# Preparing attention's keys, values and masks inside the retention chunks of a two-block transformer kernel on one Trainium2 core

## The reference

```python
r_q, r_k = rotary(r_q), rotary(r_k)                  # 8 heads of 64
ret = head_group_norm(retention(r_q, r_k, r_v), ret_norm) * silu(r_g)
c_kv, k_pe = rms_norm(d_c, kv_norm), rotary(d_pe)    # latent of 128, shared rotary part of 16
dsa = sparse_attention(q_nope, q_pe, c_kv, k_pe, q_idx, k_idx, w_idx, w_uk, w_uv) * silu(d_g)
x = x + concatenate([ret, dsa]) @ w_out
```

## Time and profile before

| | us |
|---|---|
| three runs: median (lowest to highest) | 2272.81 (2270.8 to 2273.53) |
| the profiled execution, its own time | 2270.93 |
| its span, first to last instruction | 2269.1 |
| outside the span | 1.83 |
| retention block | 85.04 |
| preparation of attention | 32.21 |
| attention's steps up to 2040 us | 140.05 |

### The profile page before, as it was taken

How to read it: one execution, slowest core, us unless ns; L and a number is a source line. 1 busy time by engine, 2 the same in 40 slices (tenths; PEclk the granted TensorE clock), 3 DMA queues, 4 the chain that set the end, 5 groups by cost and what they waited for, 6 DMA issues and landing times. The chain is left out here.

```text
span 2269.1 us, 27732 instructions
## 1 busy us (share of the span) xinstructions
PE 2117.0 (93%) x10549; PEld 1599.9 (71%) x10549; DVE 1278.9 (56%) x2211; ACT 733.0 (32%) x1292; POOL 435.1 (19%) x501
## 2 busy tenths in 40 slices
PE   7998999995969999999999998889999868989998
PEld 4744464484858888888888886856888764658876
DVE  6591895278864333223454324478999577762433
ACT  2222021122113323223444223356121335761415
POOL 2900011042310000000000001223666440300210
PEclk8999999997989999999999999899999889999999
DMA  8543110003233333334434232122211002003101
GB/s 325 155 134 116 42 46 1 0 2 121 75 102 93 93 97 89 90 106 147 121 111 130 81 97 87 58 56 61 66 47 50 20 3 81 2 25 130 51 0 75
DMA packets 187512, 180.59 MB, mean 80 GB/s; under 512 B 12982, under 2 KB 157686, under 8 KB 184074
## 3 DMA queue, kind: packets, MB, share of 16 engines
q1 hardware_dynamic: 184426, 168.61, 23.9%
q0 software_dynamic: 2880, 10.49, 1.2%
q10 hardware_dynamic: 96, 0.02, 0.0%
HBM read 165.18 MB, written 12.60 MB: 78 GB/s over the span
## 5 line engine op out<-in xcount | busy, mean ns | idle before, releaser
L1800 DVE TENSOR_TENSOR ff_part<-ff_raw,ff_part 128x1024 fp32r<-128x1024 f32 (+2 forms) x152 | 164.9, 1085 | 435.5 <-ACT ff_part L1708 435.5
L1708 ACT ACTIVATE ff_part<-ff_raw 128x1024 fp32r<-128x1024 f32 (+2 forms) x152 | 144.0, 948 | 433.4 <-PE ps L1598 430.9
L1596 PE MATMUL ps<-h,ff_part 128*128 128x512 f32 x704 | 275.5, 391 | 4.7 <-DVE ff_part L1800 4.7
L1598 PE MATMUL ps<-h,ff_part 128*128 128x512 f32 x704 | 274.7, 390 | 0.0
L1597 PE MATMUL ps<-h,ff_part 128*128 128x512 f32 x704 | 274.7, 390 | 0.0
L2416 DVE TENSOR_SCALAR_CACHE_REDUCE pj_junk<-NM,prm 128x384 uint8<-128x384 f32 (+1 forms) x186 | 163.7, 942 | 1.1
L1596 PEld LDWEIGHTS ps<-h,ff_part 128*128 128x128 f32 x704 | 132.8, 189 | 32.3 <-DVE ff_part L1800 5.1
L1596 PE MATMUL ps<-pj_part,h 128*128 128x512 f32 x384 | 153.2, 399 | 0.2 <-ACT PJ L2273 0.2
L1597 PEld LDWEIGHTS ps<-h,ff_part 128*128 128x128 f32 x704 | 132.8, 189 | 27.4
L1598 PEld LDWEIGHTS ps<-h,ff_part 128*128 128x128 f32 x704 | 132.6, 188 | 27.6
L1597 PE MATMUL ps<-pj_part,h 128*128 128x512 f32 x384 | 150.4, 392 | 0.0
(11 more groups left out here) (601 smaller groups left out, 4057.7 us busy)
## 6 DMA issues: line engine op xcount, KB each, us to landing
ff_raw<-in_w_ffn_in SPq DMA_DIRECT2D x88, 512.0 KB, 3.7
s_wm<-in_w_mod SPq DMA_DIRECT2D x16, 1024.0 KB, 4.9
pj_raw<-in_w_in SPq DMA_DIRECT2D x64, 256.0 KB, 2.7
ff_raw<-in_w_ffn_out SPq DMA_DIRECT2D x32, 384.0 KB, 3.4
ff_raw<-in_w_ffn_out SPq DMA_DIRECT2D x32, 320.0 KB, 3.0
mod_w<-in_w_mod SPq DMA_DIRECT2D x8, 1024.0 KB, 8.9
mod_x<-in_x SPq DMA_DIRECT2D x8, 512.0 KB, 13.9
w_out<-in_w_out SPq DMA_DIRECT2D x4, 1024.0 KB, 8.7
```

What stands on the lines that cost most here:

```text
L1596: nc.tensor.matmul(out, w[0], x[0], start=first, stop=False)
L1598: return nc.tensor.matmul(out, w[1], x[0], start=False, stop=last)
L1708: nc.scalar.activation(part[s % 2][0][:, 0:n, :], raw[s][:, 0:n, :], ACT.Copy).then_inc(hi, 1)
L1800: v.tensor_tensor(part[s % 2][1][:, 0:n, :], raw[s][:, 0:n, :], part[s % 2][0][:, 0:n, :].bitcast(F32), ALU.subtract).then_inc(lo, 1)
```

## The change

The preparation of attention moves into the retention block.

- At retention's start, PE transposes the attention queries (`turn_queries`) and the latent and rotary part (`turn_latent`) of all 8 tiles. ACT copies the queries out, DVE the latent and rotary part (one copy of 128 x 256 a tile). `intra`, `xi` and the gain row are loaded after the last query transposes, into the `D_Q` slab; `zeta`, `decay`, `w_uv` and the 8 pieces of `w_uk` before them.
- In each chunk PE also makes a value piece (`prepare(2 * i)`, before the state update) and a key piece (`prepare(2 * i + 1)`, after it), through bank 2, and ACT copies each out (`prepared`).
- DVE makes mask 7 before the chunks, then one of nine parts (masks 6, 5 and 4, three each) at the end of each chunk's work, the ninth after the last norm. ACT lowers masks 7, 6 and 5 after chunks 1, 4 and 7, and mask 4 at the block's end.
- The state's decay goes from DVE (one instruction) to ACT (four of 128 x 128).
- Zero-padded queries and values are gone: scores are 8 products on 64 rows, the output's second part 8 products of 64 columns. Keys are weighed by zeta in place, and the norm's squares go into the `R_K` slab.
- In `stage_first_end` pairs of weight loads share a semaphore.

The diff, cut to what the text speaks of:

```diff
             def split(k):
-                act.wait_ge(w_in[k], 32)
+                act.wait_ge(w_in[k // 2], 64)
                 nc.scalar.activation(K.mixed[k][0][:], raw[k][:], ACT.Copy).then_inc(K.pj["hi"], 1)
...
+        link(v.tensor_tensor_scan(run[:, 0:n], flag[:, 0:n], flag[:, 0:n], 0.0, ALU.add, ALU.max))
+    else:
+        link(v.scalar_tensor_tensor(out=run[:, 0:n], in0=run[:, 0:n], scalar=need, in1=flag[:, 0:n], op0=ALU.is_le, op1=ALU.mult))
+        return v.scalar_tensor_tensor(out=x, in0=x, scalar=at, in1=run[:, 0:n], op0=ALU.is_gt, op1=ALU.add)
...
+            sp.dma_start(zeta, I["zeta"]).then_inc(S["const"], 16)
+            sp.dma_start(decay, I["decay"]).then_inc(S["const"], 16)
+            with nc.allow_non_contiguous_dma(reason="latent to partitions"):
+                sp.dma_start(wuv[:], I["w_uv_2"][0].rearrange("h c d -> c h d")).then_inc(S["wuv"], 16)
+            sp.wait_ge(S["clear"], 2)
+            for h in range(AH):
+                sp.dma_start(uk[AD * (h % 2) + PE_D:AD * (h % 2 + 1), h // 2, :], I["w_uk_2"][0, h]).then_inc(S["uk"], 16)
+            sp.wait_ge(S["dqt"], NT)
             sp.dma_start(intra[:], I["intra"].rearrange("p (j a) t -> p j a t", a=2)).then_inc(S["const"], 16)
             sp.dma_start(xi[:], I["xi"]).then_inc(S["const"], 16)
-            sp.dma_start(zeta, I["zeta"]).then_inc(S["const"], 16)
-            sp.dma_start(decay, I["decay"]).then_inc(S["const"], 16)
             sp.dma_start(row[:], I["ret_norm_2"].to_broadcast([P, HALF])).then_inc(S["const"], 16)
...
             def turn(i):
                     pe.wait_ge(S["qkr"], 2 * i)
-                    pe.wait_ge(S["dqr"], i)
-                for b, slab in enumerate((R_Q, R_K, D_Q)):
+                for b, slab in enumerate((R_Q, R_K)):
                     for j in range(J):
                         tr = nc.tensor.transpose(K.bank[b][:, j * P:(j + 1) * P], K.PJ[:, slab, i, j * P:(j + 1) * P], K.ident[:])
                     tr.then_inc(S["tr"], 1)
+            def turn_queries(i):
+                if i >= 4:
+                    pe.wait_ge(S["dqr"], i - 3)
+                for j in range(J):
+                    tr = nc.tensor.transpose(K.bank[2 + i % 4][:, j * P:(j + 1) * P], K.PJ[:, D_Q, i, j * P:(j + 1) * P], K.ident[:])
+                tr.then_inc(S["dqt"], 1)
+
+            def turn_latent(i):
+                if i >= 2:
+                    pe.wait_ge(S["latr"], i - 1)
+                b = K.bank[6 + i % 2]
+                nc.tensor.transpose(b[:, 0:P], K.MS[:, i, 0:LAT], K.ident[:])
+                nc.tensor.transpose(b[:, P:2 * P], K.MS[:, i, M_PE:M_PE + P], K.ident[:]).then_inc(S["turn"], 1)
+
+            def prepare(n):
+                if n:
+                    pe.wait_ge(S["prer"], n)
+                b, m = K.bank[2][:], n // 2
+                if n % 2 == 0:
+                    nc.tensor.matmul(b, latT[:, m * P:(m + 1) * P], wuv[:].rearrange("p h d -> p (h d)"), start=True, stop=True).then_inc(S["pre"], 1)
+                else:
+                    c = slice(m % 2 * HALF, (m % 2 + 1) * HALF)
+                    nc.tensor.matmul(b, ukT[:, m // 2, :], latT[:, c], start=True, stop=False)
+                    nc.tensor.matmul(b, spread[:].rearrange("p a d -> p (a d)"), peT[:, c], start=False, stop=True).then_inc(S["pre"], 1)
+
             turn(0)
+            for i in range(NT):
+                turn_queries(i)
+                turn_latent(i)
+            pe.wait_ge(S["uk"], 16 * AH)
+            pe.wait_ge(S["dqr"], NT)
+            pe.wait_ge(S["latr"], NT)
+            for j in range(J):
+                tr = nc.tensor.transpose(K.bank[2][:, j * P:(j + 1) * P], uk[:, j, :], K.ident[:])
+            tr.then_inc(S["ukr"], 1)
             for i in range(NT):
                 for j in range(J):
-                    mm = nc.tensor.matmul(K.bank[3 + j // 2].rearrange("p (j a t) -> p j a t", j=2, a=2)[:, j % 2], kT[s][:, j, :], qpad[s][:, j, :, :],
-                                          start=True, stop=True)
+                    for a in range(2):
+                        d = slice(RD * a, RD * (a + 1))
+                        mm = nc.tensor.matmul(K.bank[3 + a][:, j * P:(j + 1) * P], kT[s][d, j, :], qT[s][d, j, :], start=True, stop=True)
                 mm.then_inc(S["smm"], 1)
                 if i + 1 < NT:
                     turn(i + 1)
+                if i == 0:
+                    pe.wait_ge(S["wuv"], 16)
+                    pe.wait_ge(S["ukr"], 2)
+                    pe.wait_ge(S["spread"], 2)
+                prepare(2 * i)
+                if i + 1 < NT:
                     pe.wait_ge(S["kzr"], i + 1)
                     if i:
                         pe.wait_ge(S["state"], i)
                     for j in range(J):
-                        mm = nc.tensor.matmul(K.bank[7][:, j * P:(j + 1) * P], rkz[s][:, j, :], K.PJ[:, R_V, i, j * P:(j + 1) * P],
+                        mm = nc.tensor.matmul(K.bank[7][:, j * P:(j + 1) * P], K.PJ[:, R_K, i, j * P:(j + 1) * P], K.PJ[:, R_V, i, j * P:(j + 1) * P],
                                               start=True, stop=True)
                     mm.then_inc(S["upd"], 1)
+                prepare(2 * i + 1)
                 pe.wait_ge(S["prob"], i + 1)
-                pe.wait_ge(S["vr"], i + 1)
                 if i:
                     pe.wait_ge(S["xqr"], i + 1)
                     pe.wait_ge(S["state"], i)
@@ -2498,7 +2575,9 @@
                     if i:
                         nc.tensor.matmul(o, xq[s][:, j, :], state[s][:, j, :], start=True, stop=False)
                     for a in range(2):
-                        mm = nc.tensor.matmul(o, prob[s][:, j, a, :], vpad[s][:, j, a, :], start=(i == 0 and a == 0), stop=(a == 1))
+                        d = slice(RD * a, RD * (a + 1))
+                        mm = nc.tensor.matmul(o[:, d], prob[s][:, j, a, :], K.PJ[:, R_V, i, (2 * j + a) * RD:(2 * j + a + 1) * RD],
+                                              start=(i == 0), stop=(i == 0 or a == 1))
                 mm.then_inc(S["out"], 1)
...
-                act.wait_ge(S["tr"], 3 * i + 3)
                 nc.scalar.activation(qT[i % 2][:], q, ACT.Copy).then_inc(S["qkr"], 1)
-                for a in range(2):
-                    d = slice(RD * a, RD * (a + 1))
-                    nc.scalar.activation(qpad[i % 2][d, :, a, :], q[d], ACT.Copy)
                 nc.scalar.activation(kT[i % 2][:], k, ACT.Copy).then_inc(S["qkr"], 1)
-                for a in range(2):
-                    d = slice(RD * a, RD * (a + 1))
-                    last = nc.scalar.activation(vpad[i % 2][:, :, a, d], K.PJ[:, R_V, i, :].rearrange("p (j a d) -> p j a d", a=2, d=RD)[:, :, a, :], ACT.Copy)
-                last.then_inc(S["vr"], 1)
-                nc.scalar.activation(K.dqT[:, :, i * P:(i + 1) * P], K.bank[2][:].rearrange("p (j t) -> p j t", j=J), ACT.Copy).then_inc(S["dqr"], 1)
...
+
+            def prepared(n):
+                act.wait_ge(S["pre"], n + 1)
+                m = n // 2
+                dst = K.kfT[:, m // 2, m % 2 * HALF:(m % 2 + 1) * HALF] if n % 2 else K.val[:, m, :]
+                nc.scalar.activation(dst, K.bank[2][:], ACT.Copy).then_inc(S["prer"], 1)
...
             take(0)
+            for i in range(NT):
+                take_queries(i)
+            act.wait_ge(S["ukr"], 1)
+            nc.scalar.activation(ukT[:], K.bank[2][:].rearrange("p (j r) -> p j r", j=J), ACT.Copy).then_inc(S["ukr"], 1)
             for i in range(NT):
                 if i + 1 < NT:
                     take(i + 1)
+                prepared(2 * i)
+                if 0 < i < NT - 1:
+                    act.wait_ge(S["state"], i)
+                    for j in range(J):
+                        last = nc.scalar.activation(state[1 - i % 2][:, j, :], state[i % 2][:, j, :], ACT.Copy, scale=decay[:, j:j + 1])
+                    last.then_inc(S["dec"], 1)
+                prepared(2 * i + 1)
                 if i:
                     root(i - 1)
                 act.wait_ge(S["out"], i + 1)
                 nc.scalar.activation(K.PJ[:, R_Q, i, :], K.bank[5 + i % 2][:], ACT.Copy).then_inc(S["oev"], 1)
             root(NT - 1)
+            lower(4)
...
-            for x in (*qpad, *vpad, *state):
+            g.memset(spread[:], 0.0).then_inc(S["clear"], 1)
+            g.memset(uk[:], 0.0).then_inc(S["clear"], 1)
+            pool.wait_ge(S["latr"], NT)
+            for x in state:
                 g.memset(x[:], 0.0).then_inc(S["zero"], 1)
             pool.wait_ge(S["const"], 80)
             for i in range(NT):
                 s = i % 2
                 if i + 1 < NT:
-                    if i >= 2:
-                        pool.wait_ge(S["upd"], i - 1)
-                    g.tensor_tensor(rkz[s][:].rearrange("p j (a d) -> p (j a) d", a=2), K.PJ[:, R_K, i, :].rearrange("p (h d) -> p h d", h=RH),
-                                    zeta.unsqueeze(2).to_broadcast([P, RH, RD]), ALU.mult).then_inc(S["kzr"], 1)
```

(30 more changed lines are left out.)

160 lines of the change are left out of this document (68 added, 92 removed).

## The result

The changed kernel took 2259.85 us (median of 4 runs, 2259.59 to 2260.80), the kernel before 2272.96 (4 runs, 2270.80 to 2273.53): a ratio of 0.9949, 95% interval 0.9936 to 0.9961. The prediction was 2261.7 us, with 2252 to 2268 as its range.

A forecast was written before the change was run, and what follows sets the result against it. Retention was taken as bound by a ring of DVE's norm, POOL's product and weighed keys, PE's update and DVE's addition. Removing 32.2 us, adding 19.3 and 1.8, gave -11.1: 2261.7 us, range 2252 to 2268.

The forecast's parts named there:

- entry, to chunk 1's addition: Retention's start: transposes, latent copies, mask 7 and POOL's held products delay chunk 1's addition by 7.6 us (bounds +3.9, +11.4).
- five rounds: Chunk 1's to chunk 6's addition: mask parts holding POOL lengthen the ring by 6.1 us (bounds -1.5, +10).
- tail, to the block's end: Last addition to retention's end: remaining mask parts, mask 4's picks and a held product add 5.6 us (bounds +3.5, +7).
- preparation: The stretch between retention and attention, all on the path: its 32.2 us go away.
- attention's start: First logits run at PE's low clock, after about 10 us of idleness at retention's end: +1.8 us.
- The pairs of loads in the first end: First end's paired semaphores: second load issued 1 us later, hidden by a later wait on POOL; 0, bounds 0 and +0.5.
- the holding: DVE's mask parts and POOL's products exclude each other in the ring; counted as one product, 1.25 us, per instruction at entry.
- The open point: Whether a DVE scan holds POOL throughout; assumed yes, rounds +6.1 us, or +2.6 if it read only one stream.
- ACT's decay: Ready about 9.2 us after the previous update, asked for at 10 to 11: covered by 1 us.
- A: Rival, no holding in the ring: retention lengthens by only 5.9 us, total -24.5, 2248.3 us; chance 0.19.
- B: Rival, ring waits for PE or ACT: 5.5 to 11 us more over seven rounds, about 2270 us; chance 0.12.
- C: Rival, PE at the low clock for most of each chunk: slower, 2289 us at three quarters; chance 0.05.

The follow-up runs named there:

- a2: Changed kernel with masks 6 and 5 also made before the chunks and equally long one-input DVE counts in place of their parts in the rounds: 2271.35 us, ratio 1.0000.
- a3: Changed kernel with masks 6 and 5 also made before the chunks and nothing in place of their parts in the rounds: 2270.79 us, ratio 0.9996.
- a0: The changed kernel measured and profiled once more, unedited: 2258.09 us, ratio 0.9946 to the kernel before.
- a4: Changed kernel with the state's decay back on DVE as one instruction instead of four on ACT: 2258.59 us, ratio 0.9941.
- d1: Changed kernel with mask 7 first in DVE's work and all query transposes ahead of the latents': 2255.65 us, ratio 0.9930.
- b4: Changed kernel with 11 unread matmuls behind PE's last retention output, to keep PE busy: 2256.42 us, ratio 0.9936.
- b3: Kernel before the change, with POOL weighing a chunk's keys one chunk earlier: 2268.57 us, ratio 0.9990.
- c3: Changed kernel with keys weighed one chunk ahead, the decay back on DVE and 18 unread matmuls behind the last retention output: 2260.92 us, ratio 0.9957.
- a1: Changed kernel with POOL weighing the keys one chunk ahead, before its wait for the norm: 2251.29 us, ratio 0.9911.
- b1: Changed kernel with 18 unread matmuls behind PE's last retention output, to keep PE busy: 2261.98 us, ratio 0.9961.
- d2: Changed kernel with keys weighed one chunk ahead, mask 7 first with queries turned before latents, and 11 unread matmuls: 2247.30 us, ratio 0.9891.
- d3: Same three edits as d2, but mask 7's running count placed in the unused space of attention's keys: 2248.63 us, ratio 0.9896.

## Why the prediction was right, step by step

Held against the stretch of 254.0 and 241.3 us:

| step | predicted | measured |
|---|---|---|
| entry, to chunk 1's addition | +7.6 | +9.3 |
| five rounds | +6.1 | +5.25 |
| tail, to the block's end | +5.6 | +3.2 |
| preparation | -32.2 | -32.15 |
| attention's start | +1.8 | +1.65 |
| sum | -11.1 | -12.7 |

The sum comes closer than its terms by some luck: the entry cost 1.7 us more than forecast, rounds and tail together 3.2 us less. In the other profile of the changed kernel the rounds are +4.4. The pairs of loads in the first end, priced at 0, cost some 0.3, inside their bounds: from the first to the last start of DVE's work there (L2056) 29.5 us pass before and 29.8 in both profiles after. One range in the prediction's working is off: -26 to -4 is the sum of the bounds without the 1.8 us of attention's start; with it they give -24.5 to -2.

**Rounds.** The mechanism was the forecast's, and a2 and a3 show it: without the holding the rounds fall by 2.1 us against before, where the lower bound had 1.5. The gaps from norm to addition were 5.85 (scan), 5.4 (picks), 4.1 (part 0), 5.9 (scan) and 5.1 (picks), against 5.7, 5.9, 4.4, 5.4 and 5.65: in this profile the scans cost more than forecast and the picks less, which cancels in part (in a0 the second scan's gap is 5.1 too). The open point was the scan. The trace of before does have one beside POOL, which the prediction missed, in attention: 128x384, begun at 1940.82 while POOL's product ran until 1941.11, 1.11 us long, where the scans in the preparation, 1.49 us for 640 columns and 0.27 more for every 128, give an estimate of 0.95 for 384. It points to holding, over too short an overlap to size it. After the change the scan holds POOL for its whole length. The Trainium skill, SBUF — State Buffer, section "SBUF: two separate sides", had ruled so for a DVE instruction with two SBUF inputs; the trace agrees, 2.85 us instead of 1.27 for the product beside the scan, and 1.28 beside a count with one input. Two updates behind the scans took 1.69 and 2.02 us instead of 1.16, after PE had waited 2.96 and 1.94 us, a term that I had not counted; in a0 only the first did.

**Entry.** Two terms were mis-sized. The low clock at the block's start lasted 6 us (0.50 granted from 1784.60 to 1790.60, 0.98 in the next 2 us), not 3, so the latent copies ended 9.75 us after the block's start instead of 8.7; and chunk 1's addition waited 1.98 us for ACT's decay, which I had priced as covered. The holding of mask 7's picks and mask 6's first part, which I had at 1.25 each, came to 0.8 to 0.9 each (2.09 and 2.17 instead of 1.28 for the picks). a4 confirms the wait: without it 1.2 to 1.3 us less. d1, with mask 7 first, brings 2.2 to 2.3 us less, but it changes the order and the holding together, so it sizes neither; the length of the low clock is read from the trace and was not tried.

**Tail.** The mechanism was right and the term too large by 2.4 us. Norm and addition in the last rounds no longer met POOL as in the earlier trace rows (L2573 and L2574 there lost 1.57 us between them; in the last two norms after the change they take 0.33 to 0.44 and 0.69), so that holding, priced at +0.6, came to -1.1 us. After the last norm came 2.0 us more instead of 2.5. The two mask parts cost their 3.3 us, and the 0.8 us of waiting was gone, both as forecast.

**Attention's start.** The first logits took 3.78 us, and b4, where PE hardly idles, gives 1.99 and 2.1 to 2.6 us back: shown. The +1.65 of the table is the whole of attention, 138.5 against 136.8 us; b4's 135.9 lie under both, and 0.8 us of what is between b4 and the kernel before is the second group of logits, 2.78 us against 3.61 in the earlier trace rows.

**Rivals.** A (no holding) is out by a2 and a3. B (PE or ACT) appeared in part: the wait for ACT's decay at chunk 1, 2 us, and PE's low clock in the two updates, 1.4 us (0.6 in a0). The prediction had the decay ready about 9.2 us after the update before it: where nothing holds the ring (a2, a3), every second round lasts 9.23 us instead of 9.09, and its addition waits for the decay last. b3 shows that the kernel before had PE and ACT close behind its ring. C did not come: the granted clock over the five rounds was 0.94, against 0.93 before. As for the decay on ScalarE, the prediction costed it at nothing, and in the change as made it is (a4); that it carries some 5 us as soon as the ring is shortened, only c3 showed.

## What to carry to other kernels

Before work is moved into an engine's waits, list which instructions of its new neighbours it holds up, and whether anybody waits for those: here the same DVE microseconds cost 6.5 to 7.3 us as scans and picks beside products on the ring, and nothing as counts with one SBUF input. Then look for the step that stands in the ring without need (the weighed keys behind the product): taking it out was worth 5 to 8.5 us after the change and 2 to 3 before it. And price an edit in the company of the others: the decay's engine was worth nothing alone and some 5 us with the keys ahead.

## What the runs showed of the hardware that was not expected

- Tiny instructions are held too: the norm's `tensor_scalar` on 128x8 takes 0.17 us alone, 0.55 to 0.72 beside POOL's products and keys in a1 (L2682) and 0.71 in the earlier trace rows.
- When DVE and POOL hold each other in turn, both pay: around mask 7's picks each instruction of either side took 2.1 to 2.25 us (1.28 and 1.27 alone), one waiting for the other each time.
- Four decays of 128x128 on ACT take 1.28 us together, 0.32 each, near the lower of the two bounds (0.2 and 0.6).
- After PE had been kept busy, its second group of logits, 2.65 us of idleness later, took 2.78 us in b4, 3.27 in b1, 3.10 in c3 and 1.99 in d2 and d3; in the changed kernel it took 3.79, in a1 2.65. The clock in the rounds does not decide it, since it was 1.00 in c3 as in d3. What does was not tried.
